# A mixer and expert network in one kernel: the expert stage rebuilt around ranked experts and light blocks, block copies on GpSimd

## The chip, the cores and the metric

One core of a Trainium2 chip runs the whole program. The metric is the device time of one execution in microseconds; the time of the kernel before is the median of 3 runs. Engines are called PE (TensorE), DVE (VectorE), ACT (ScalarE), GpSimd (POOL in the profile) and SP (SyncE).

## What is computed

The reference takes 256 tokens of width 1024 through two blocks. The first (two layers of a SwiGLU network, a mixer of a short convolution and a gated recurrence, and another SwiGLU network) and the attention and recurrence of the second are not touched. The change is in the last part of the second block, a hierarchical mixture of 16 experts:

```python
g_logits = hf @ w_rg + b_rg
g_top = argmax(g_logits)                      # one of 4 groups
e_in = (hf @ w_re + b_re)[group g_top]        # its 4 experts
top_v, top_j = lax.top_k(e_in, 2)             # two experts a token
for e in range(16):
    he = silu(hf @ w1[e]) * (hf @ w3[e])      # 1024 -> 512
    y = y + combine[:, e:e + 1] * (he @ w2[e])  # 512 -> 1024
x = x + g2 * y
```

All is fp32. So 512 rows (256 tokens, 2 experts each) are to be worked on, spread over 16 experts as the data have it; the kernel must be right for every spread.

## The kernel before

Every fp32 product of weights is taken as three products of fp32r halves: hi x hi, hi x lo, lo x hi. Weights come from memory in units of 1 MB (128 x 2048). For a unit ACT writes the rounded half (`expert_hi`, L1124) and DVE the remainder (`expert_lo`, L1544: raw minus hi). Six raw buffers (RAWS) and four pairs of split buffers (SPLITS) are used in turn: a fetch waits for the split that frees its raw buffer, a split waits until PE has used the unit four before.

An expert has six units: 0 and 1 for w1, 2 and 3 for w3, 4 and 5 for w2. The order of units interleaves two neighbours: the four of block b come, then the last two of block b - 1 (`expert_unit`).

Routing. After the norm, PE computes the router's logits, DVE picks group and experts, PE counts and ranks by a product with a triangular matrix (L861 to L865), and DVE makes from it each row's place among the 512 rows sorted by expert (L1620 to L1632). One-hot matrices of these places (`first_one_hot`) select the rows: PE multiplies the split hidden states with them (`gather`, L882), ACT and DVE write the outcome to `xsel` (`select`, L1161 and L1716), transposed, hi and lo, 512 columns. The first 256 columns are made before the first product, the other 256 within block 0.

Blocks. There are 19 blocks of 128 slots: one for each expert in the order of numbers, and three extra ones for experts with more than 128 rows, whose numbers and offsets DVE works out during blocks 1 to 3 (`extra_counts`, `extra_places`, `extra_experts`). The weights of the 16 first blocks lie in a known order, so their fetches begin before the routing is known; the three extra ones are fetched by an index that SP reads. GpSimd copies a block's 128 columns from `xsel` (at an offset that it reads from `offs`) to one of two buffers in `xT` (`columns`, L609); block 0 is taken from `xsel` itself.

On PE the order is, for block b: units 0 and 1 (gate, bank 0), the turn of the hidden rows of block b - 1 (four transposes, L908), units 2 and 3 (up, bank 1), then the outputs of block b - 1 (units 4 and 5, L926 to L928, banks 3 and 4). A unit of a product is 12 matmuls of 512 columns (L897 to L899). ACT takes the silu (L1174), DVE the product with up (L1791), ACT and DVE split the turned hidden rows (L1186, L1782), and ACT and DVE write the output rows to `ybuf` (L1202, L1808; DVE multiplies its half by the gate vector). GpSimd stores `ybuf` to `yd` in memory (L591). At the end, GpSimd gathers each token's two rows from `yd` by index (L624), and DVE adds them with their weights (`near_sum`); rows of the last two blocks (FAR and FAR + 1) are not gathered but added by a product with one-hot shares (`far_products`, L946).

`idle(n)` and `keep_busy(n)` on PE are matmuls on zeros between these steps.

Of the kernel before, what the change touches and what calls it, by code (L numbers as in the profile page):

```python
# [23 lines left out]
I32 = mybir.dt.int32  # L24
# [40 lines left out]
EXTRA = (2 * T) // (SLOTS + 1)  # L65
BLOCKS = EXPERTS + EXTRA
BATCH = 2 * SLOTS
BATCHES = 2
LAST_OFFSET = 2 * T - SLOTS
# [3 lines left out]

FAR = BLOCKS - 2
FAR_SLOT = FAR * SLOTS
# [3 lines left out]
PICK_FILL, PLACE_FILL = 20, 12  # L79
# [23 lines left out]
def constants():  # L103
# [12 lines left out]
            "c_before": (s < t).astype(np.float32), "c_iota": np.arange(BATCH, dtype=np.float32)}  # L116
# [53 lines left out]
def expert_unit(b, j):  # L170

    if j < 4:
        return j + (6 * b - 2 if b else 0)
    return 6 * b + (4 + j if b < BLOCKS - 1 else j)


UNIT_OF = {expert_unit(b, j): (b, j) for b in range(BLOCKS) for j in range(6)}
assert sorted(UNIT_OF) == list(range(6 * BLOCKS))  # L180
# [7 lines left out]
def build(nc, t, out):  # L188
    ctx = ExitStack()
    with ctx:  # L190
# [55 lines left out]
        def xT_banks(i):  # L246
# [94 lines left out]
        before = sb("before", [P, P], F32, route)  # L341
        iota = sb("iota", [P, BATCH], F32, route)
        counts = sb("counts", [P, 8, EXPERTS], F32, route)
        extra = sb("extra", [P, 3, EXTRA, EXPERTS], F32, route)
# [6 lines left out]
        emap = sb("emap", [P, EXTRA], I32, route)  # L351
# [8 lines left out]
        oneh0 = sb("oneh0", [P, TT, BATCH], F32R, moe)  # L360
        far = sb("far", [P, TT, 2], F32, moe)
        share = sb("share", [P, 2, TT, SLOTS], F32, moe)
        tests = sb("tests", [P, 2, BATCH], F32, moe)
        oneh1 = sb("oneh1", [P, TT, BATCH], F32R, moe)
# [11 lines left out]
        oneh = [oneh0, oneh1]  # L376
# [5 lines left out]
        xcur = [xT[:, 4 * n:4 * n + 4].rearrange("p k a t -> p (k a t)").rearrange("p (m s) -> p m s", s=SLOTS)  # L382
                for n in range(2)]
# [64 lines left out]
            "rw_hi rw_split routeT_ps routeT route_ps rexp_in rexp rexp2_in rexp2 "  # L448
            "tables_in h2_hi h2_lo picked rank_ps begins extras xcur slots weighed oneh0 oneh "
# [45 lines left out]
        def stored_to(b):  # L495


            return 16 * (b // 2 + 1)
# [22 lines left out]
        def sp_block2(sp):  # L521
            for p in range(6 * BLOCKS):
                b, j = UNIT_OF[p]
# [10 lines left out]
                if b < EXPERTS:  # L534
                    src = t["experts"][b * 6 + j:b * 6 + j + 1, :, :]
                else:
                    if j == 0:
                        if b == EXPERTS:
                            sp.wait_ge(ev["extras"], 1)
                            expert = 0  # L540
                        m = b - EXPERTS
                        expert, last = sp.value_load(emap[0:1, m:m + 1], min_val=0, max_val=EXPERTS - 1), expert
                    e = expert if j < 4 or b == BLOCKS - 1 else last
                    src = t["experts"][bass.ds(e * 6 + j, 1), :, :]
# [8 lines left out]
        def pool_block2(pool):  # L553
# [31 lines left out]
            g = nc.gpsimd  # L585

            def store(b):

                pool.wait_ge(ev["y_left"], b + 1)
                pool.wait_ge(ev["y_right"], b + 1)  # L590
                pool.dma_start(t["yd"][b * SLOTS:(b + 1) * SLOTS, :], ybuf[:, b % 2, :]).then_inc(stored[b % 2], 16)  # L591
# [6 lines left out]
            def columns(b):  # L598


                pool.wait_ge(*((ev["begins"], 1) if b < EXPERTS else (ev["extras"], 1)))
                offset = pool.value_load(offs[0:1, b:b + 1], min_val=0, max_val=LAST_OFFSET)
                if b == 1:
                    pool.wait_ge(xT_ps, XT_DONE + 8 * BATCHES)
                    pool.wait_ge(xThi_done, XT_DONE + 4 * BATCHES)
                    pool.wait_ge(xTlo_done, XT_DONE + 4 * BATCHES)
                if b >= 3:
                    pool.wait_ge(*expert_used(expert_unit(b - 2, 3) + 1))
# [2109 lines left out]
```

## Time and profile before

| | us |
|---|---|
| runs (3) | 1888.61, 1890.15, 1888.44; median 1888.61 |
| profiled execution, first to last instruction | 1885.4 |
| PE busy | 1815.4 (96%) |
| DVE busy | 1446.7 (77%) |
| ACT busy | 982.6 (52%) |
| GpSimd busy | 118.2 (6%) |

For the profiled execution the profile has its span alone; the runs lie 3.0 to 4.8 us above it. Times within the kernel are counted from the span's start. The expert stage is its last fifth. The clock column of a stretch is the TensorE clock that was granted, 1.00 for 2.4 GHz and 0.50 for 1.2 GHz. A group's "idle before" is time in which the engine stood still ahead of these instructions, and behind the arrow stands what ended it.

### The profile page before, as it was taken

Reading aid. Unit: us, or ns where it says so; the run is one execution under the profiler, and the core shown is the slowest. Engines: PE = TensorE matmul, PEld = TensorE weight load, DVE = VectorE, ACT = ScalarE, POOL = GpSimd, SP = SyncE. Lnnn points to the kernel's source line nnn. Section 1 sums busy time; section 2 is a strip of 40 time slices with the busy share of each in tenths; the row PEclk is TensorE's granted clock in tenths of the full one; section 3 lists DMA queues with packets and bytes.
Section 4 is the critical chain, followed back from the end, with each engine's and each line's share of the span. In section 5 each row is a group of like instructions: output and inputs, shape, how many; then the busy total and the mean of one; then the engine's idle time right before and its main releaser. Section 6 shows DMA issues by size and latency. Waiting matters only on the chain.

```text
span 1885.4 us, 28170 instructions
## 1 busy us (share of the span) xinstructions
PE 1815.4 (96%) x10912; PEld 1597.0 (85%) x10912; DVE 1446.7 (77%) x1543; ACT 982.6 (52%) x932; POOL 118.2 (6%) x116
## 2 busy tenths in 40 slices
PE   7999999999999999999999999998998899999998
PEld 6888899998888788889999978886997777777876
DVE  7555786857877765567877687779588889999998
ACT  4444465534444454446464345443435456767774
POOL 1000000000000000000000000001000011212222
PEclk9999999999999999999999999998999999999999
DMA  6555455564777465545546557774432359999995
GB/s 250 190 188 196 161 179 179 201 224 144 280 252 259 157 216 185 200 156 181 199 164 245 176 186 279 248 260 144 140 136 90 103 185 373 367 373 391 389 385 217
DMA packets 61615, 417.14 MB, mean 221 GB/s; under 512 B 7288, under 2 KB 7664, under 8 KB 13648
## 3 DMA queue, kind: packets, MB, share of 16 engines
q1 hardware_dynamic: 51392, 369.19, 54.4%
q0 software_dynamic: 10112, 46.59, 7.3%
q8 instruction: 70, 1.15, 0.2%
q14 instruction: 25, 0.20, 0.0%
q10 hardware_dynamic: 16, 0.01, 0.0%
HBM read 405.79 MB, written 9.98 MB: 221 GB/s over the span
## 4 chain that ended last, share of the span: by engine, by line
PE 80%; DVE 11%; DVEq 3%; issue 3%; ACT 1%; ACTq 1%; DMA 0%; POOL 0%; POOLq 0%
PE ps L1916 14%; PE ps L1915 7%; PE ps L1900 7%; PE ps L1902 7%; PE ps L1901 7%; PE ps L2017 4%; PE ps L2018 4%; PE ps L2021 4%; PE ps L899 3%; PE ps L897 3%; PE ps L898 3%; PE ps L926 2%; PE ps L1913 2%; DVE wlo L2350 2%; PE ps L928 2%
## 5 line engine op out<-in xcount | busy, mean ns | idle before, releaser
L2350 DVE TENSOR_TENSOR wlo<-raw,whi 128x2048 fp32r<-128x2048 f32 x236 | 538.2, 2289 | 194.0 <-ACT whi L2182 191.2
L2182 ACT ACTIVATE whi<-raw 128x2048 fp32r<-128x2048 f32 x236 | 451.1, 1912 | 271.6 <-PE ps L1902 112.7
L1916 PE MATMUL ps<-xT,whi 128*128 128x512 f32 x1232 | 440.4, 397 | 0.0
L1915 PE MATMUL ps<-xT,wlo 128*128 128x256 f32 x1232 | 344.6, 280 | 0.1
L1916 PEld LDWEIGHTS ps<-xT,whi 128*128 128x128 f32 x1232 | 231.9, 188 | 47.6
L1900 PE MATMUL ps<-xT,whi 128*128 128x256 f32 x928 | 263.5, 284 | 2.0 <-DVE xT L2361 2.0
L1901 PE MATMUL ps<-xT,whi 128*128 128x256 f32 x928 | 263.2, 284 | 0.0
L1902 PE MATMUL ps<-xT,wlo 128*128 128x256 f32 x928 | 263.1, 284 | 0.0
L1915 PEld LDWEIGHTS ps<-xT,wlo 128*128 128x128 f32 x1232 | 233.0, 189 | 8.9 <-DVE xT L2369 1.0
L1544 DVE TENSOR_TENSOR wlo<-raw,whi 128x2048 fp32r<-128x2048 f32 x76 | 201.3, 2661 | 10.6 <-ACT whi L1124 9.9
L2206 ACT ACTIVATE rest<-ps 128x512 f32<-128x512 f32 x88 | 52.7, 599 | 251.9 <-PE ps L1916 251.9
L1900 PEld LDWEIGHTS ps<-xT,whi 128*128 128x128 f32 x928 | 178.8, 193 | 2.2 <-DVE xT L2361 2.2
L1901 PEld LDWEIGHTS ps<-xT,whi 128*128 128x128 f32 x928 | 178.8, 193 | 0.0
L1902 PEld LDWEIGHTS ps<-xT,wlo 128*128 128x128 f32 x928 | 178.7, 193 | 0.0
L1124 ACT ACTIVATE whi<-raw 128x2048 fp32r<-128x2048 f32 x76 | 145.6, 1918 | 47.9 <-PE ps L928 30.5
L2017 PE MATMUL ps<-whi,hhi 128*128 128x512 f32 x288 | 112.4, 390 | 2.1 <-DVE wlo L2350 2.1
L897 PE MATMUL ps<-whi,xT 128*128 128x512 f32 x288 | 113.9, 395 | 0.0
L899 PE MATMUL ps<-whi,xT 128*128 128x512 f32 x288 | 112.4, 390 | 0.0
L898 PE MATMUL ps<-wlo,xT 128*128 128x512 f32 x288 | 112.2, 390 | 0.0
L2018 PE MATMUL ps<-wlo,hhi 128*128 128x512 f32 x288 | 112.1, 389 | 0.0
L1544 DVE TENSOR_TENSOR wlo<-mod,whi 128x2048 fp32r<-128x2048 f32 x38 | 87.4, 2299 | 2.3 <-ACT whi L1124 2.2
L2021 PE MATMUL ps<-whi,hlo 128*128 128x512 f32 x288 | 88.7, 389 | 0.0
(516 smaller groups left out, 3288.1 us busy)
## 6 DMA issues: line engine op xcount, KB each, us to landing
raw<-stream SPq DMA_DIRECT2D x236, 1024.0 KB, 4.9
raw<-experts SPq DMA_DIRECT2D x76, 1024.0 KB, 7.2
mod<-experts SPq DMA_DIRECT2D x38, 1024.0 KB, 6.7
adaraw<-ada POOLq DMA_DIRECT2D x24, 1024.0 KB, 5.1
yd<-lnrow POOLq DMA_DIRECT2D x17, 512.0 KB, 8.7
lnrow<-ln_g POOLq DMA_DIRECT2D x6, 512.0 KB, 4.8
lnrow<-ln_b POOLq DMA_DIRECT2D x6, 512.0 KB, 6.3
x_sb<-x SPq DMA_DIRECT2D x1, 1024.0 KB, 5.1
```

The source lines that it names most:

```text
L897: mm(o, h, wh[:, rs], start=k == 0, stop=False)
L899: last = mm(o, lo, wh[:, rs], start=False, stop=k == KD - 1)
L1544: v.tensor_tensor(splits[p % SPLITS][1], raws[p % RAWS], splits[p % SPLITS][0].bitcast(F32), ALU.subtract).then_inc(lo_done, 1)
L1900: nc.tensor.matmul(outs[tile], wh, xh[:, k, :], start=k == 0, stop=False)
L1901: nc.tensor.matmul(outs[tile], wh, xl[:, k, :], start=False, stop=False)
L1902: last = nc.tensor.matmul(outs[tile], wl, xh[:, k, :], start=False, stop=k == KD - 1)
L1915: nc.tensor.matmul(bank(b, T), wl, xThi[:, k, :], start=False, stop=False)
L1916: return nc.tensor.matmul(bank(b), wh, both, start=False, stop=k == KD - 1)
L2017: nc.tensor.matmul(o, h, whi[:, slot, c:c + 512], start=start and k == 0, stop=False)
L2018: nc.tensor.matmul(o, h, wlo[:, slot, c:c + 512], start=False, stop=False)
L2182: act_fn(whi[:, slot, :], raw[:, slot, :], ACT.Copy).then_inc(hi_done, 1)
L2350: v.tensor_tensor(wlo[:, slot, :], raw[:, slot, :], whi[:, slot, :].bitcast(F32), ALU.subtract).then_inc(lo_done, 1)
```

## The change

The expert stage is rebuilt. The experts are ranked by their counts: the expert of rank r has at most min(256, 512 / (r + 1)) rows. So it is fixed how many blocks each rank needs, and how wide: ranks 0 and 1 have two blocks of 128 slots, rank 2 one of 128 and one of 64, ranks 3 to 6 one of 128, ranks 7 to 15 one of 64. These are 9 wide and 10 light blocks for 16 experts, and each expert's weights are fetched once, by an index that SP reads after the sort. RANK_AT gives the order in which ranks are worked on: 0, 7, 8, 9, 1, 10, 11, 12, 2, 13, 14, 15, 3, 4, 5, 6.

In a light block a stationary tile holds 64 columns of the hi half and 64 of the lo half side by side, and two matmuls (with the hi and the lo weights) take the place of three; the two halves of the outcome's partitions are added later, for gate and up by an fp32 matmul with two stacked unit matrices (`fold`), for the rows out by ACT and DVE. Both batches of `gather` come before the first product. GpSimd copies the columns of all blocks, of block 0 too, into three buffers (two in `xT`, one in the one-hot matrices' place), in the order columns(q + 2), then the stores of expert q.

```diff
+LIGHT = 64
+RANK_AT = [0, 7, 8, 9, 1, 10, 11, 12, 2, 13, 14, 15, 3, 4, 5, 6]
+def rows_at_most(rank):
+
+    return min(T, 2 * T // (rank + 1))
+def widths(q):
+
+    left = rows_at_most(RANK_AT[q])
+    out = []
+    while left > 0:
+        out.append(LIGHT if left <= LIGHT else SLOTS)
+        left -= out[-1]
+    return out
...
+COLUMNS_AT = {0: (0, 1), 4: (0, 1), 8: (0, 1), 1: (2,), 2: (0,), 3: (2,), 5: (2,), 6: (0,), 7: (2,), 9: (2,), 10: (0,),
+              11: (2,), 12: (0,), 13: (1,), 14: (0,), 15: (1,)}
-PICK_FILL, PLACE_FILL = 20, 12
+PICK_FILL, PLACE_FILL, FIRST_FILL = 20, 20, 12
...
         def sp_block2(sp):
+                if j == 0:
+                    if q == 0:
+                        sp.wait_ge(ev["sorted"], 1)
+                        expert = 0
+                    expert, last = sp.value_load(emap[0:1, q:q + 1], min_val=0, max_val=EXPERTS - 1), expert
+                e = expert if j < 4 or q == EXPERTS - 1 else last
+                src = t["experts"][bass.ds(e * 6 + j, 1), :, :]
                 sp.dma_start(raws[p % RAWS], src.rearrange("o p n -> p (o n)")).then_inc(expert_loaded(p)[0], 16)
...
+            def columns(q):
+                if q == 0:
+                    pool.wait_ge(ev["begins"], 1)
                     pool.wait_ge(xThi_done, XT_DONE + 4 * BATCHES)
                     pool.wait_ge(xTlo_done, XT_DONE + 4 * BATCHES)
+                for n, m, width in BLOCKS_OF[q]:
+                    of = q if m == 0 else EXPERTS + RANK_AT[q]
+                    offset = pool.value_load(offs[0:1, of:of + 1], min_val=0, max_val=2 * T - width)
+                    users = [b for b in range(n) if BUFFER_OF[b] == BUFFER_OF[n]]
+                    if users:
+                        pool.wait_ge(*expert_used(expert_unit(BLOCK[users[-1]][0], 3) + 1))
+                    nc.gpsimd.tensor_copy(xcur(n), xsel[:, :, :, bass.ds(offset, width)]).then_inc(ev["xcur"], 1)
+
+            columns(0)
             columns(1)
+            for q in range(EXPERTS):
+                if q + 2 < EXPERTS:
+                    columns(q + 2)
+                for n, _, _ in BLOCKS_OF[q]:
+                    if n < FAR:
+                        store(n)
...
+            def product(q, j):
+                for n, m, width in BLOCKS_OF[q]:
+                    o = bank((G_BANK if j < 2 else U_BANK)[m])
+                    for r in range(4):
+                        k = 4 * (j % 2) + r
+                        rs = slice(r * D_EXPERT, (r + 1) * D_EXPERT)
+                        if width == SLOTS:
+                            h, lo = (xcur(n)[:, part, k, :] for part in range(2))
+                            mm(o, h, wh[:, rs], start=k == 0, stop=False)
+                            mm(o, h, wl[:, rs], start=False, stop=False)
+                            last = mm(o, lo, wh[:, rs], start=False, stop=k == KD - 1)
+                        else:
+                            both = light_columns(n, k)
+                            mm(o, both, wh[:, rs], start=k == 0, stop=False)
+                            last = mm(o, both, wl[:, rs], start=False, stop=k == KD - 1)
...
+            def turn_hidden(n):
+                    pe.wait_ge(silu_done, FFN_DONE + n + 1)
+                    pe.wait_ge(ev["ucopy"], LIGHT_NO[n] + 1)
+                    for a, rows_in_two in enumerate((gated, hide)):
+                        for f in range(4):
+                            c = (4 * a + f) * LIGHT
+                            last = mm(o[:, c:c + LIGHT], rows_in_two[:, f * P:(f + 1) * P], fold, start=True, stop=True)
...
+            for c in range(BATCHES):
+                for group in range(8):
+                    gather(c, group)
+            idle(FIRST_FILL)
+            for q in range(EXPERTS + 1):
+                if q >= 1:
+                    turn_hidden(first_block(q - 1))
+                if q < EXPERTS:
+                    pe.wait_ge(ev["xcur"], last_block(q) + 1)
...
+                    product(q, 0)
+                    product(q, 1)
...
+                if q >= 1 and len(BLOCKS_OF[q - 1]) > 1:
+                    turn_hidden(last_block(q - 1))
+                if q < EXPERTS:
+                    product(q, 2)
+                    product(q, 3)
+                if q >= 1:
+                    outputs(q - 1, 4)
+                    outputs(q - 1, 5)
...
+            def block_offsets():
+                v.tensor_tensor(sort2[:, :, :], perm[:, :, :], across_q(begin), ALU.mult)
+                dve.drain()
+                v.tensor_reduce(begin_q, sort2[:, :, :], AX_X, ALU.add)
+                dve.drain()
+                v.tensor_tensor(offs[:, 0:EXPERTS], begin_q, last_at, ALU.min)
...
+            first_one_hot(1)
+            block_offsets()
+            for pair in range(4):
+                select(1, pair)
+            for p in range(SPLITS):
+                expert_lo(p)
...
+            def turned_hidden(n):
+                dve.wait_ge(ev["silT"], LIGHT_NO[n] + 1)
+                both, product = light_hidden(m), hide[:, 0:4 * LIGHT]
+                v.tensor_tensor(product, gated[:, 0:4 * LIGHT], bank(T_BANK[m], 4 * LIGHT, 8 * LIGHT),
+                                ALU.mult).then_inc(hid_done, 1)
+                dve.drain()
...
+                v.tensor_copy(both[:, 0], product).then_inc(hhi_done, 1)
+                dve.drain()
+                v.tensor_tensor(both[:, 1], product, both[:, 0].bitcast(F32), ALU.subtract).then_inc(hlo_done, 1)
+            def rows_out(n):
+                if width == LIGHT:
+                    dve.wait_ge(ev["y_left"], n + 1)
+                    v.tensor_tensor(ybuf[0:LIGHT, n % 2, :], ybuf[0:LIGHT, n % 2, :], banks(Y_BANK[m], 2)[0:LIGHT, :],
+                                    ALU.add).then_inc(ev["y_right"], 1)
...
-                if half == 0:
-                    v.tensor_tensor(acc, acc, row(mod, 5)[:, cs], ALU.mult)
-                    dve.drain()
+                v.tensor_tensor(acc, acc, row(mod, 5)[:, cs], ALU.mult)
+                dve.drain()
```

The sort itself is two comparisons of all pairs of experts (16 x 16 = 256 elements) and their sums on DVE, between the counts and the first one-hot matrix; the steps for second blocks follow in the rounds of experts 1 to 4, the shares of far rows in rounds 10 and 11. The splits of units 0 to 3 on ACT and DVE, which stood within the norm and the routing, come after both batches. DVE's order in the round of expert q is: the turned hidden rows of expert q - 1, two splits, routing work, a split, the product rows of expert q, a split, a split, the rows out of expert q - 1, a split.

## Rows read from the trace of the kernel before

**Rows 1.** Busy time by stretch (count), clock, DMA share, GB/s.

```profile
1550.11:1690.50 140.39, 131.29 (x582) 105.45 (x581) 134.91 (x106) 98.61 (x70) 26.80 (x14) 1.00 0.98 368
1690.50:1850.00 159.50, 157.09 (x696) 126.27 (x695) 154.05 (x83) 118.28 (x82) 33.53 (x18) 1.00 1.00 390
```

**Rows 2.** Waits, 1550 to 1850 us: total us, times, longest.

```profile
PE ps L926 <- issue: 10.2, 15, 1.4
DVE wlo L1544 <- ACT whi L1124: 9.2, 32, 0.4
```

**Rows 3.** Timeline of DVE, one block: start us, us, engine, line, operation.

```profile
1709.60 2.29 DVE L1544 TENSOR_TENSOR wlo<-raw,whi 128x2048 fp32r<-128x2048 f32 x1 [0.20 <-ACT whi L1124]
...
1711.81 0.68 DVE L1808 TENSOR_TENSOR lnrow<-ps,mod 128x512 f32<-128x512 f32 x1
1712.89 6.22 DVE L1544 TENSOR_TENSOR wlo<-raw,whi 128x2048 fp32r<-128x2048 f32 x2 [0.39 <-ACT whi L1124]
...
1724.04 0.67 DVE L1791 TENSOR_TENSOR mod<-mod,ps 128x512 f32<-128x512 f32 x1
...
1727.11 2.29 DVE L1544 TENSOR_TENSOR wlo<-raw,whi 128x2048 fp32r<-128x2048 f32 x1 [0.20 <-ACT whi L1124]
```

**Rows 4.** GpSimd's copies: first two together (timeline), all (duration ns min/median/max).

```profile
1541.51 5.85 POOL L609 CAST xT<-xsel 128x2048 fp32r x2 [48.11 <-DVE xsel L1716]
...
L609 POOL CAST xT<-xsel x18: 1914/3228/3981, 1541.5 to 1836.0; 128x2048 fp32r x18
```

**Rows 5.** Timeline of PE: first product, block 17, outputs.

```profile
1528.94 0.47 PE L897 MATMUL ps<-whi,xsel 128*128 128x512 f32 x1 [0.83 <-ACT xsel L1161]
...
1849.95 0.39 PE L897 MATMUL ps<-whi,xT 128*128 128x512 f32 x1
...
1855.40 0.60 PE L936 MATMUL ps<-eye,tests 128*128 128x128 f32 x4
1855.84 0.60 PE L908 MATMUL ps<-eye,mod 128*128 128x128 f32 x4
...
1861.75 0.39 PE L926 MATMUL ps<-whi,hThi 128*128 128x512 f32 x1
```

**Rows 6.** Timeline of PE, fp32 matmuls of 64 columns, after a gap and later.

```profile
1456.79 1.09 PE L771 MATMUL ps<-eye,lnrow 128*128 128x128 f32 x8 [3.32 <-ACT lnrow L1076]
1459.10 3.67 PE L779 MATMUL ps<-av,qk 128*128 128x64 f32 x16 [1.22 <-DVE xT L1406]
...
1479.57 1.89 PE L779 MATMUL ps<-av,qk 128*128 128x64 f32 x16
```

**Rows 7.** Timeline of DVE between the counts and the first product.

```profile
1520.03 0.19 DVE L1620 TENSOR_TENSOR_SCAN counts<-ones,ps 128x16 f32<-128x16 f32 x1 [0.47 <-PE ps L865]
...
1523.42 1.22 DVE L1606 TENSOR_TENSOR xT<-cat,xT 128x1024 fp32r<-128x1024 f32 x1
...
1528.15 0.69 DVE L1716 CAST xsel<-ps 128x512 fp32r<-128x512 f32 x1 [0.27 <-PE ps L882]
```

**Rows 8.** Timeline of the end: PE and SP.

```profile
1867.35 0.60 PE L908 MATMUL ps<-eye,mod 128*128 128x128 f32 x4
...
1880.33 2.91 SPq L550 DMA_DIRECT2D out<-x_sb  x4
```

**Rows 9.** DVE by shape: busy us, mean ns, idle before.

```profile
L1464 DVE TENSOR_TENSOR cat<-ps,nrm 128x256 f32<-128x256 f32 x2 | 0.8, 420 | 0.1
...
L1643 DVE TENSOR_SCALAR mod<-iota,sit 128x256 f32<-128x256 f32 x2 | 0.6, 349 | 0.1
...
L1475 DVE COPY qk<-ps 128x512 f32<-128x512 f32 x2 | 1.3, 686 | 0.6 <-PE ps L771 0.6
...
L1394 DVE TENSOR_TENSOR lg<-ps,score 128x1024 f32<-128x1024 f32 x2 | 2.4, 1222 | 0.1
```

**Rows 10.** DMA, 1550 to 1850 us: all, and the fetches of a unit.

```profile
DMA packets 16777, 113.96 MB, mean 380 GB/s; under 512 B 1854, under 2 KB 1854, under 8 KB 3902
...
raw<-experts SPq DMA_DIRECT2D x67, 1024.0 KB, 7.2
```

More of the change, by code:

```diff
@@ L521, in sp_block2 @@
         def sp_block2(sp):
-            for p in range(6 * BLOCKS):
-                b, j = UNIT_OF[p]
+            for p in range(6 * EXPERTS):
+                q, j = UNIT_OF[p]
                 if p < RING:
@@ new lines, in act_block2 @@
+            for c in range(BATCHES):
+                for pair in range(4):
+                    select(c, pair)
+            for p in range(SPLITS):
+                expert_hi(p)
+            for q in range(EXPERTS + 1):
+                two = q >= 1 and len(BLOCKS_OF[q - 1]) > 1
+                if q >= 1:
+                    turned_hidden(first_block(q - 1))
+                if two:
+                    gate_rows(last_block(q - 1))
+                if q < EXPERTS:
+                    freed(q, 0)
+                    freed(q, 1)
+                if two:
+                    turned_hidden(last_block(q - 1))
+                if q < EXPERTS:
+                    gate_rows(first_block(q))
+                    if q == EXPERTS - 1:
@@ L1665, in extra_counts @@
                 dve.drain()
-                v.tensor_tensor_scan(counts[:, 6, :], ones[:, 0:EXPERTS], many, 0.0, ALU.mult, ALU.add)
+                v.tensor_reduce(begin_q, sort2[:, :, :], AX_X, ALU.add)
                 dve.drain()
-            def extra_places():
-                for m in range(EXTRA):
-                    v.scalar_tensor_tensor(extra[:, 0, m, :], counts[:, 6, :], float(m + 1), many, ALU.is_equal, ALU.mult)
-                v.scalar_tensor_tensor(counts[:, 7, :], counts[:, 6, :], float(SLOTS), off_x, ALU.mult, ALU.subtract)
+                v.tensor_tensor(offs[:, 0:EXPERTS], begin_q, last_at, ALU.min)
@@ L1720, in dve_block2 @@
                 select(0, pair)
-            expert_lo(2)
             first_one_hot(1)
-            expert_lo(3)
+            block_offsets()
+            for pair in range(4):
+                select(1, pair)
+            for p in range(SPLITS):
+                expert_lo(p)
             def weights():
@@ new lines, in dve_block2 @@
+            for q in range(EXPERTS + 1):
+                two = q >= 1 and len(BLOCKS_OF[q - 1]) > 1
+                if q >= 1:
+                    turned_hidden(first_block(q - 1))
+                if two:
+                    product_rows(last_block(q - 1))
+                if q < EXPERTS:
+                    freed(q, 0)
+                    freed(q, 1)
+                if two:
+                    turned_hidden(last_block(q - 1))
+                if q == 1:
+                    steps_of_first_blocks()
+                elif q == 2:
+                    steps_of_second_blocks()
+                elif q == 3:
+                    choice_rows()
+                elif q == 4:
@@ L2567, in _ @@
             dve.drain()
+            dve.wait_ge(eye_in, 16)
+            v.tensor_tensor(fold, eye[:, 0:LIGHT], eye[:, LIGHT:], ALU.add)
             dve.wait_ge(bada_in, 16)
```

458 lines of the change are left out of this document (237 added, 221 removed).

## The prediction

> **What bounds the kernel now.** I read the table by stretch first, then the waits, then one block on VectorE (DVE), then PE, GpSimd and the DMA. The expert stage runs from PE's first product at 1528.94 us to 1867.35, where the last block's hidden rows are turned: 338.4 us for 18 of 19 rounds [rows 5, 8]. In it PE, DVE and DMA are all nearly full [rows 1]: no engine has much room, and only less work can make it shorter. What paces a round is DVE. Between two equal points of successive blocks (1709.60 and 1727.11) lie 17.5 us [rows 3], filled by six splits of weights at 2.2 us, three pieces of block work at 0.61, 1.7 us by which GpSimd's copy lengthens a split (the pair takes 6.22 where two alone take 4.5), and 0.6 us of waits for ACT. The same copy takes 3.23 us by the median [rows 4]. In the first half, where small routing work lies between the splits, PE is busy 131.3 of 140.4 us, later 157.1 of 159.5 [rows 1], and its waits stand at the outputs [rows 2]. PE needs 12 matmuls of 512 columns a unit: 24 in 5.45 us is 0.228, and at the outputs 0.233 [rows 5]; I take 0.2314, so 2.78 us a unit, and 16.7 a block with 0.45 for the turn, close behind DVE's 17.5. DMA moves 380 GB/s there and 1 MB lands in 7 us [rows 10]; nobody waits for it.
>
> **What the change does, part by part.** Removed: the three extra experts' 18 units (114 become 96). There are 9 wide blocks of 128 slots and 10 light ones of 64. A light block needs 8 matmuls a unit, where a wide one needs 12. Added: two blocks in experts 0 and 4 (both wide) and 8 (wide and light) of the new order, a sort of experts before the first fetch, fp32 matmuls against the fold in every light block, more DVE work in a light block, and a first expert that waits for both of its copies.
>
> **Cost of one expert.** PE, wide: 16.7 + 0.45. PE, light: 48 x 0.2314 = 11.1, and eight fp32 matmuls of 64 columns; eight such took 1.89 us at full clock [rows 6], so 13.0. PE, two wide: 5.55 us a unit, 33.3. DVE, light: six splits 13.3; a 512-wide copy out of PSUM 0.61; product, copy and difference at 256 wide, 0.42, 0.35 and 0.42 with their drains 1.3; a 1024-wide add with PSUM 1.15 [rows 9], each less the 0.07 by which neighbours overlap; together 3.05. The copy of 64 slots is half of the wide one, so I take half its toll, 0.9 (0 if it falls beside other work, 1.7 at most). Sum 17.2: **a light expert is DVE-paced**, and saves PE time that nobody needs. A double expert is PE-paced. Lights cost no less than a wide block did before; what is won is that three whole rounds go, and part of it goes back to the doubles.
>
> **Schedule of the stage,** counted from the first product. Four split units stand between DVE and PE, so DVE enters each light run with a lead and lags PE in each double.
> Expert 0's products: 4 x 5.55 = 22.2.
> Experts 1 to 4: the fourth split in the ring ends 4.1 later (a split of ACT 1.9 and of DVE 2.2 after the unit is freed). DVE then has expert 1's round: 13.3, block work 3.65 (two blocks of expert 0), toll 0.9, routing steps with 256-wide operations 2.2, so 20.0; expert 2's: 13.3 + 3.05 + 3.4 for two wide copies + 1.0, so 20.7. In the next round it needs 11.2 until PE has turned block 3 (light work 1.3, three splits 6.6, routing 0.8, copy 0.6, fold 1.9), then PE is alone on the path: 22.2 for expert 4's products and 3.7 for expert 3's outputs. Sum 81.9.
> Experts 5 to 8: DVE lags 6.1 behind, 1.6 and 0.5 of waits, rounds of 18.8 and 18.9, 10.4 until the turn, 4 x 4.63 + 3.7 for the double with one light block. 78.5.
> Experts 9 to 12: 6.1 + 1.0, rounds of 19.0, 19.2 and 19.2 (the shares of far rows, 1.2 each, and wide copies), then 1.3 + 4.4 + 1.9, so 72.0. Experts 13 to 15 are wide, at the 17.5 of now: 52.5.
> Sum 22.2 + 81.9 + 78.5 + 72.0 + 52.5 = 307.1, against 338.4: **31.3 won**.
>
> **The start.** Fetches no longer run ahead. From the counts (1520.03) to the last copy of the gathered rows now takes until 1528.84, and the first product follows [rows 7]. The sort adds five dependent 256-wide steps and a cast, less what now lies there: 1.7 us; two splits that no longer stand ahead of the routing give 0.35 back. So the first gather ends at 1530.2. The second one-hot (six 256-wide operations, 2.2 [rows 9]) and the second gather (5.4, as from 1523.42 to 1528.84) must now come before the first product: 1537.8. Then GpSimd reads its offset (0.3) and copies two wide blocks, which took 5.85 together beside splits [rows 4]: first product at about 1544.0, 15.1 later. The first unit is issued on SP at about 1524, so its landing (7 us) and split hide behind this; with that cover gone it would cost up to 8. The twelve fillers on PE last 2.8, so about 3.3 us are idle. After such a gap (3.32) the clock went to half and the same matmuls took 3.67 where 1.89 is full [rows 6]. I take 3 us for it, bounds 0 and 5. A copy by itself takes 1.91 at least [rows 4]; two of those instead of 5.85 give the low bound, 2 us earlier.
> On this copy the Trainium skill (GPSIMD Engine Reference, Elementwise — side-by-side cycle accounting and Engine selection) says that one-input work runs near line rate there, 1.03 cycles an element; at 1.2 GHz a wide copy would be an estimated 1.8 us, and the start 2 us earlier. The trace agrees only with its shortest copy; beside splits the measurement decides.
>
> **The end.** From the last turn (1867.35) to the end of the span 18.05 us are left; its last instructions are the stores of the output [rows 8]. The gate factor is now applied in all four near sums, two more 512-wide products of 0.69 [rows 9] and a drain ahead of the last rows out of PSUM, 1.5 in all: 19.55. The store of rows and the gathers keep their place; no price.
>
> **Sum against the profiled span of 1885.4:** +15.1 (start) + 3 (clock) - 31.3 + 1.5 = -11.7, so 1873.7. The runs shown lie 3.0 to 4.8 above that span, their median 3.2; so 1888.6 - 11.7 = 1876.9. A measurement of this kernel can tell about 0.2% (3.8 us) from no change.
>
> **The rivals.**
> *The ring gives no lead (slower).* Place: the hand-over from a double expert to the lights. DVE works in program order, and in the double it also waits for PE before each piece. If it comes out of a double without split units in hand, the four units (8.8 us) of each of three light runs are paid again: +26, or 1903. It decides from 12 us lost, less than half of the lead. For: all DVE work is in one queue, and PE already waited at its outputs when DVE had a little more to do [rows 2]. Against: PE's units are 5.55 us there, DVE's and ACT's 4.1. 0.12.
> *The clock falls in the light runs (slower).* PE is busy 13.0 of 17.2 us there, with gaps up to 1.7. If every light expert ran at half clock it would need 26 and pace the run, 9 x 9 = +80; PE would then be full, which brings the clock back, so I take a third, +27: 1904. For it speaks the fall after the 3.32 us gap [rows 6]; against, that no single gap is as long. 0.06.
> The Trainium skill (TensorE: Matmul & The Clock Gate, HAM oscillation) tells of a kernel whose bursts shorter than their waits fell back to the low clock at every tile; the gap in the trace agrees, and no row shows it for gaps as short as these.
> *DVE is cheaper than I say (faster).* The copies fall into its idle time in the doubles, half tolls vanish (10 x 0.9), the light work is 2.5 instead of 3.05 (5) and the clock stays up (3): -17, or 1860. For: in the doubles DVE has 20 to 30 us to spare. Against: copies come after the rows are stored, at the head of a round. 0.16.
> *The wins just cover the start (no change).* A first product 5 us later than I say, and a quarter of the no-lead case (6.5): 1888.4. 0.14.
>
> **How the numbers follow.** The forecast (1866 to 1885) has 0.52. Faster by over 0.2%, so under 1884.8: 0.52 + 0.16 = 0.68. Within: 0.14. Slower: 0.12 + 0.06 = 0.18. The predicted time is the first case's, 1877. The range 1857 to 1896 reaches the cheap-DVE case and the middle of the no-lead case, and takes in the bounds of tolls (9 each way), start (2 to 8) and clock.
>
> **What would show it.** Right: 96 splits of DVE; first product near 1544 after two copies; products of expert 0 in 22.2 us; in light runs DVE has hardly any idle time and PE idles a quarter; a light expert every 17 us; in doubles DVE waits for ACT, and ACT for PE. Wrong: light experts at 15 us or below, or at 20 and more; PE's clock under 1.0 within them; ACT waiting for DMA; a first product before 1540 or after 1550.

## The result and the profile after

The changed kernel takes 1901.74 us (median, 1900.68 to 1902.75), the kernel before 1888.53 (1887.86 to 1890.15): a ratio of 1.0071, interval 1.0059 to 1.0083. The forecast of 1877 and its range (1857 to 1896) were wrong, and so was the sign. The profiled span is 1900.7 us, against 1885.4 before.

The start first. Timelines of DVE, GpSimd and PE of the changed kernel (start us, us, engine, line, operation):

```profile
1522.38 0.17 DVE L1747 SCALAR_TENSOR_TENSOR counts<-ps,sorts 128x16 f32<-128x16 f32 x1 [0.25 <-PE ps L933]
...
1540.10 0.69 DVE L1862 CAST xsel<-ps 128x512 fp32r<-128x512 f32 x1 [0.36 <-PE ps L950]
...
1541.87 5.81 POOL L677 CAST xT<-xsel 128x2048 fp32r x2 [44.89 <-issue]
...
1547.74 0.70 PE L967 MATMUL ps<-whi,xT 128*128 128x512 f32 x1 [4.92 <-POOL xT L677]
```

The counts stand at 1522.38, 2.35 us later than in [rows 7]. The kernels of the experiments, which compute the same up to there, have them at 1518.3 to 1522.0, so most of this is the spread between executions. From the counts to the first product it is 25.4 us, where the forecast had 1544.0 - 1520.03 = 24.0. The two wide copies take 5.81 together, as in [rows 4]. So, from the counts on, the start is as forecast but for 1.4 us.

The stage, from that product to the last turn at 1882.71, took 335.0 us against 338.4 before and 307.1 forecast. This is the table by stretch (us, busy us of PE, of its weight loads, DVE, ACT and GpSimd with counts, granted clock, DMA share, GB/s). Experts are counted from 0 in the new order. The stretches end where the first block of expert 4, of 8, of 12 and of 15 is turned:

```profile
1547.74:1660.33 112.59, 102.42 (x440) 82.51 (x441) 84.06 (x70) 58.16 (x42) 13.88 (x10) 0.94 0.78 282
1660.33:1747.69 87.36, 75.82 (x330) 60.76 (x329) 68.92 (x52) 53.47 (x40) 11.40 (x10) 0.92 0.84 306
1747.69:1825.46 77.77, 69.04 (x301) 55.63 (x300) 69.85 (x54) 54.68 (x41) 11.92 (x9) 0.91 0.89 329
1825.46:1882.71 57.25, 53.22 (x233) 43.31 (x233) 49.35 (x28) 37.40 (x27) 29.66 (x9) 0.97 0.84 319
```

The forecast had 104.1, 78.5, 72.0 and 52.5 for them: each is 5 to 9 us longer. Against [rows 1], DVE has fallen from nearly full to 0.75 to 0.90 of a stretch, the clock from 1.00 to as low as 0.91, and DMA from 368 and 390 GB/s to between 282 and 329. So the work did get less, and no engine is full over a whole stretch any more: something is waited for. At a clock of 0.94, 0.92, 0.91 and 0.97, twice what is missing is half clock (1.2 instead of 2.4 GHz): 13.5 + 14.0 + 14.0 + 3.4 = 45 us of the stage.

The waits name it. First the list for 1550 to 1850 us (total, times, longest), then PE's timeline at the places:

```profile
DVE wlo L1662 <- ACT whi L1215: 45.5, 18, 6.1
ACT whi L1215 <- PE ps L969: 44.7, 16, 10.0
...
PE ps L993 <- DVE mod L1924: 10.0, 6, 3.4
...
PE ps L967 <- DVE lnrow L1958: 7.3, 2, 3.7
```

```profile
1633.11 0.68 PE L967 MATMUL ps<-whi,xT 128*128 128x512 f32 x1 [3.66 <-DVE lnrow L1958]
1633.59 0.63 PE L968 MATMUL ps<-wlo,xT 128*128 128x512 f32 x1
...
1637.30 0.40 PE L969 MATMUL ps<-whi,xT 128*128 128x512 f32 x1
...
1667.98 1.09 PE L986 MATMUL ps<-eye,mod 128*128 128x128 f32 x4 [3.39 <-DVE mod L1920]
...
1722.98 0.77 PE L967 MATMUL ps<-whi,xT 128*128 128x512 f32 x1 [3.67 <-DVE lnrow L1958]
...
1755.34 1.91 PE L993 MATMUL ps<-spt,mod 128*128 128x64 f32 x11 [3.40 <-DVE mod L1924]
...
1847.07 0.50 PE L967 MATMUL ps<-whi,xT 128*128 128x512 f32 x1 [4.02 <-POOL xT L677]
```

In [rows 2] DVE waited 9.2 us for ACT, here 45.5; and ACT waits 44.7 for PE to free a unit. PE itself waits at five places of 3.4 to 4.0 us: before the products of experts 4 and 8 for the stored rows, before the turn of the second block of each for its product rows, and once, at expert 14, for GpSimd. Behind the first of them a product starts every 0.43 us instead of every 0.23, for some 3.5 us. The same happens in light experts, behind shorter waits:

```profile
1607.86 2.33 PE L993 MATMUL ps<-spt,mod 128*128 128x64 f32 x16 [1.71 <-DVE mod L1924]
...
1610.52 0.63 PE L973 MATMUL ps<-wlo,onehs 128*128 128x512 f32 x1
```

Where DVE stands idle is seen when the stage is cut into its light runs and its double experts (the same columns as above; first light run, the double expert 4, last light run):

```profile
1577.10:1633.11 56.01, 47.22 (x212) 37.86 (x213) 52.37 (x46) 36.92 (x28) 7.38 (x6) 0.94 0.90 334
1633.11:1667.98 34.87, 31.48 (x132) 25.51 (x133) 20.79 (x21) 17.36 (x12) 4.89 (x4) 0.94 0.64 225
1755.34:1808.07 52.73, 48.13 (x201) 38.67 (x201) 44.99 (x37) 35.00 (x27) 6.51 (x5) 0.87 0.87 321
```

DVE is busy 0.94 and 0.85 of these light runs, and 0.60 of the double.

The wait at expert 14 is one copy, the last but one of GpSimd's copies. GpSimd's timeline, and DVE's beside it:

```profile
1796.14 2.76 POOL L677 CAST xT<-xsel 128x2048 fp32r x1
...
1814.64 2.79 POOL L677 CAST xT<-xsel 128x2048 fp32r x1
...
1832.04 14.98 POOL L677 CAST xT<-xsel 128x2048 fp32r x1
```

```profile
1830.77 2.28 DVE L1662 TENSOR_TENSOR wlo<-raw,whi 128x2048 fp32r<-128x2048 f32 x1
1832.97 0.68 DVE L1933 TENSOR_TENSOR hTlo<-ps,hThi 128x512 fp32r<-128x512 f32 x1
1833.57 2.27 DVE L1662 TENSOR_TENSOR wlo<-raw,whi 128x2048 fp32r<-128x2048 f32 x1
...
1840.17 0.67 DVE L1920 TENSOR_TENSOR mod<-mod,ps 128x512 f32<-128x512 f32 x1
...
1842.97 2.28 DVE L1662 TENSOR_TENSOR wlo<-raw,whi 128x2048 fp32r<-128x2048 f32 x1
1845.18 0.68 DVE L1961 COPY lnrow<-ps 128x512 f32<-128x512 f32 x1
1845.78 3.38 DVE L1662 TENSOR_TENSOR wlo<-raw,whi 128x2048 fp32r<-128x2048 f32 x1
```

The same copy took 2.76 and 2.79 us an expert or two earlier, and 14.98 here. In those 15 us no DVE row carries a wait, and no split is lengthened (2.27 to 2.28) until the copy out of PSUM at 1845.18, behind which the split takes 3.38 and the copy ends. Two pieces that read one operand from PSUM and one from SBUF (1832.97, 1840.17) stand in between and did not let it in. The end of the kernel is as before: 1900.7 - 1882.71 = 18.0 us from the last turn.

### The profile page after: what moved, and what is told of

Its sections match the earlier page's. It is cut to its first block, busy times and chain, and to the rows that moved or that the text cites. A ratio compares the mean times of both kernels' runs of the same rounds, so it can differ in the third digit from the quotient of the medians.

```text
span 1900.7 us, 28124 instructions
## 1 busy us (share of the span) xinstructions
PE 1802.2 (95%) x10812; PEld 1586.7 (83%) x10812; DVE 1407.2 (74%) x1555; ACT 948.1 (50%) x914; POOL 115.4 (6%) x118
## 4 chain that ended last, share of the span: by engine, by line
PE 73%; DVE 13%; DVEq 4%; issue 4%; ACT 3%; POOL 1%; ACTq 1%; DMA 0%; POOLq 0%
PE ps L2114 14%; PE ps L2113 7%; PE ps L2098 7%; PE ps L2100 7%; PE ps L2099 7%; PE ps L2215 4%; PE ps L2216 4%; PE ps L2219 4%; DVE wlo L1662 2%; PE ps L2111 2%; DVE wlo L2548 2%; PE ps L967 2%; PE ps L968 1%; PE ps L969 1%; DVE mod L2670 1%
## 5 line engine op out<-in xcount | busy, mean ns | idle before, releaser
L2548 DVE TENSOR_TENSOR wlo<-raw,whi 128x2048 fp32r<-128x2048 f32 x236 | 538.3, 2290 | 196.5 <-ACT whi L2380 194.0
L2380 ACT ACTIVATE whi<-raw 128x2048 fp32r<-128x2048 f32 x236 | 450.8, 1911 | 275.8 <-PE ps L2100 113.7
L1662 DVE TENSOR_TENSOR wlo<-raw,whi 128x2048 fp32r<-128x2048 f32 x64 | 152.2, 2380 | 41.8 <-ACT whi L1215 41.6
L2404 ACT ACTIVATE rest<-ps 128x512 f32<-128x512 f32 x88 | 52.5, 597 | 253.1 <-PE ps L2114 253.1
L1215 ACT ACTIVATE whi<-raw 128x2048 fp32r<-128x2048 f32 x64 | 122.2, 1913 | 81.2 <-PE ps L969 38.0
L1662 DVE TENSOR_TENSOR wlo<-mod,whi 128x2048 fp32r<-128x2048 f32 x32 | 73.1, 2284 | 12.1 <-ACT whi L1215 12.1
L2670 DVE SCALAR_TENSOR_TENSOR mod<-adaraw,csil_now,mod 128x512 f32 (+1 forms) x96 | 72.2, 752 | 11.1 <-issue 5.4
L2583 DVE TENSOR_TENSOR sil<-ps,rest 128x512 f32<-128x512 f32 x44 | 30.4, 692 | 62.9 <-ACT rest L2404 62.9
L967 PE MATMUL ps<-whi,xT 128*128 128x512 f32 x144 | 59.8, 415 | 16.3 <-POOL xT L677 8.9
```

Source lines behind the costliest of these rows:

```text
L1215: act_fn(splits[p % SPLITS][0], raws[p % RAWS], ACT.Copy).then_inc(hi_done, 1)
L1662: v.tensor_tensor(splits[p % SPLITS][1], raws[p % RAWS], splits[p % SPLITS][0].bitcast(F32), ALU.subtract).then_inc(lo_done, 1)
L2380: act_fn(whi[:, slot, :], raw[:, slot, :], ACT.Copy).then_inc(hi_done, 1)
L2548: v.tensor_tensor(wlo[:, slot, :], raw[:, slot, :], whi[:, slot, :].bitcast(F32), ALU.subtract).then_inc(lo_done, 1)
```

## Experiments

All are timed in 3 rounds beside the kernel before, which had medians of 1887.85 to 1888.3 us in them. They fall in two groups: the waits and the copies (e1, e3 to e10), and the clock (e2, e11 to e16). Where a recorded expectation puts the long copy at expert 15, it is the copy for expert 14.

**e1: wait only for what is read.** A double expert's second block writes banks that only the second block before it had in use; the kernel of the change waits for the rows of every block up to the one two places back, that of expert q - 2. e1 waits for the rows of the last second block alone.

```diff
-                        pe.wait_ge(ev["y_left"], first_block(q) - 1)
-                        pe.wait_ge(ev["y_right"], first_block(q) - 1)
+                        seconds = [n for n in range(first_block(q)) if BLOCK[n][1] == 1]
+                        pe.wait_ge(ev["y_left"], seconds[-1] + 1)
+                        pe.wait_ge(ev["y_right"], seconds[-1] + 1)
```

> The wait of a double expert's first product is moved from the rows of the expert two before to the rows of the last second block, which is what its banks need. Theory (the late rows cost time): in the changed kernel PE stood 3.66 and 3.67 us there, right ahead of PE-paced rounds, so both go, 7.3 us, and with them some of the half clock that follows; 1892 to 1895 against 1901.7. Rival (DVE paces these rounds, so PE only waits elsewhere): 1900 to 1902, with the waits turned up in front of the outputs.

Measured: 1889.0 us, ratio 1.0005 (0.9995 to 1.0014). That is 12.7 us under the change, more than the theory had; the rival falls. The two waits were 7.3 us. Most of the rest is the half clock behind them, by e13 below.

**e3: a narrow copy.** GpSimd copies 8 of a block's columns; the products of the others read what stood there, so that the expert outputs are left out.

```diff
-                    nc.gpsimd.tensor_copy(xcur(n), xsel[:, :, :, bass.ds(offset, width)]).then_inc(ev["xcur"], 1)
+                    nc.gpsimd.tensor_copy(xcur(n)[:, :, :, 0:8], xsel[:, :, :, bass.ds(offset, 8)]).then_inc(ev["xcur"], 1)
```

> GpSimd copies 8 columns of each block in place of all; the rest of each block is left out. Theory (copies cost at the start, by their tolls on DVE and once by standing 15 us): start 5 us earlier, 4 us at the copy of the last buffer, tolls of at most 24 us of DVE time of which about half is on the path: 1875 to 1885. Rival (copies hide, doubles and waits are all of the loss): only the start's 5 us and the 4 us go, 1892 to 1893.

Measured: 1886.29 us, ratio 0.9987 (0.9977 to 0.9996), between the two. GpSimd's timeline, and PE's behind the long copy:

```profile
1802.95 1.17 POOL L677 CAST xT<-xsel 128x128 fp32r x1
...
1819.11 13.37 POOL L677 CAST xT<-xsel 128x128 fp32r x1
...
1834.13 1.15 POOL L677 CAST xT<-xsel 128x128 fp32r x1
```

```profile
1832.54 0.50 PE L967 MATMUL ps<-whi,xT 128*128 128x512 f32 x1 [2.09 <-POOL xT L677]
```

The copy for expert 14 moves a sixteenth of the data and still stands for 13.37 us. So its length is not work; it stands still. PE waits 2.09 us for it, where it waited 4.02, and the waits for stored rows (3.7 each) and for the second blocks' product rows (3.4 each) are all there: that is what keeps e3 above its theory.

**e4, e5: the copies on ScalarE (ACT),** which leaves DVE's splits at 2.28 to 2.29 us (e8's rows below); e5 has e1's wait as well.

```diff
-                    nc.gpsimd.tensor_copy(xcur(n), xsel[:, :, :, bass.ds(offset, width)]).then_inc(ev["xcur"], 1)
...
+                    act_fn(xcur(n), xsel[:, :, :, bass.ds(offset, width)], ACT.Copy).then_inc(ev["xcur"], 1)
```

The copies of experts 0 and 1 stand before ACT's splits of units 0 and 2, those of expert q + 2 at the end of round q.

> The same copies on ACT, one round ahead, in place of GpSimd. ACT has a third of the stage idle; a wide copy should take 1.92 us there and lengthen no split. Theory (GpSimd's copies take DVE's time and once keep PE waiting): the tolls and the 4 us wait go, 1880 to 1892. Rival (the copies delay ACT's own halves of the splits, which is as bad): 1900 to 1906.

> Two parts at once: TensorE waits at experts 4 and 8 for the rows of the last second block alone (that by itself gave 1889.0), and the copies of the columns are done by ScalarE (that by itself gave 1889.2). Theory (each removed wait lies on the path, and they are different stretches of it): 1901.7 - 12.7 - 12.5 = 1876, range 1873 to 1880. Rival (TensorE goes at the pace of the splits of the weights, and whatever is taken out is waited for at the next split): 1886 to 1889.

Measured: e4 1889.24 (1.0008, 0.9998 to 1.0017), e5 1877.75 (0.9951, 0.9934 to 0.9968). Each alone is worth 12.5 to 12.7 us, both 24.0: they add up, and the theory of waits in series holds against the one of a pace that takes everything back. In e4 the first product waits for something else, the split of its weights, which now begins behind the copies:

```profile
1549.23 0.77 PE L948 MATMUL ps<-whi,xT 128*128 128x512 f32 x1 [6.97 <-DVE wlo L1663]
```

**e6: a gap for the copy.** e1, and behind DVE's split of a wide block's turned rows:

```diff
+                    dve.drain()
```

> As the wait kernel (1889.0), with GpSimd's copies, and a drain of VectorE after the split of a wide block's turned activations, so that VectorE has a gap once in each expert. Theory (a copy gets in only at a gap, and without one it stood for 15.0 us at expert 15): that copy takes 3 to 5 us, TensorE's wait of 4.0 us for it goes, and the time is 1883 to 1886. Rival (the length of that copy has another cause, or the pace there is that of the splits anyway): 1888 to 1890.

Measured: 1882.79 (0.997, 0.9959 to 0.9981), 6.2 under e1. GpSimd's copies for experts 14 and 15, and DVE beside the first:

```profile
1819.72 2.78 POOL L677 CAST xT<-xsel 128x2048 fp32r x1
...
1835.86 2.77 POOL L677 CAST xT<-xsel 128x2048 fp32r x1
```

```profile
1820.64 0.67 DVE L1934 TENSOR_TENSOR hTlo<-ps,hThi 128x512 fp32r<-128x512 f32 x1
1821.48 3.17 DVE L1663 TENSOR_TENSOR wlo<-raw,whi 128x2048 fp32r<-128x2048 f32 x1 [0.16 <-issue]
```

With a gap of 0.16 us the copy goes through: 2.78 us instead of 14.98, for 0.9 us on the next split. It is as short in the other three profiles with this drain (e9, e15, e16). Single executions scatter by 3 to 4 us, and the two profiled ones are only 2.4 apart; the 6.2 is the difference of the medians of 10 and 7 runs, which do not overlap.

**e7: the first split earlier.** e5, and ACT splits unit 0 between the two batches of gathered rows.

> As the kernel with both (e5), and ScalarE splits the first unit of weights ahead of its copies of the second batch of gathered tokens instead of behind them. In the ScalarE kernel the first product waited 6.97 us for VectorE's part of that first unit. Theory: the first product starts 3 to 4 us earlier, and all of it is kept: 3 to 4 us under e5. Rival (splits pace the stage in its first experts): under 1 us of it is kept.

Measured: 1871.66 (0.9917, 0.99 to 0.9933), 6.1 under e5; the first product is at 1542.53 instead of 1547.35, 4.8 earlier. All of it is kept; the 1.3 us beyond it are not secured, as the four runs of each kernel lie up to 5.6 us apart.

**e8, e10: the turn of a second block later.**

```diff
-                if q >= 1 and len(BLOCKS_OF[q - 1]) > 1:
-                    turn_hidden(last_block(q - 1))
                 if q < EXPERTS:
                     product(q, 2)
                     product(q, 3)
+                if q >= 1 and len(BLOCKS_OF[q - 1]) > 1:
+                    turn_hidden(last_block(q - 1))
```

> As e7, and TensorE turns the activations of a second block after the fourth unit's products of the next expert instead of between the second and the third. Theory (the waits of 3.4 us ahead of that turn at experts 5 and 9, and what there is of it at expert 1, are hand-over time that two more units hide): 6 to 9 us under e7. Rival (VectorE stands at the turn that now comes later and releases the next units later by as much): within 2 us of e7, or slower.

> The change as it stands, with nothing but the later turn of a second block. Theory (the waits are in series): 9 us under the change, 1891 to 1895. Rival (the waits of 3.7 us at experts 4 and 8 follow from the same rows, which now come later still, and take it back): 1899 to 1902.

Measured: e8 1862.23 (0.9865, 0.9848 to 0.9881), 9.4 under e7; e10, the change with this alone, 1890.9 (1.0006, 0.9994 to 1.0018), 10.8 under it (three of its ten runs lie at 1885.6 to 1886.0, seven at 1890.1 to 1893.5). In e10 the waits for the rows stay as they were (3.67 at expert 4). Something is taken back at the outputs, where PE waits 10.7 us for split weights instead of 7.2, but less than the waits for product rows that go. **e8 beats both kernels**, the one before by 26 us. Its table by stretch, cut at the same turns:

```profile
1543.13:1644.72 101.59, 96.04 (x441) 77.68 (x442) 79.89 (x70) 70.46 (x51) 2.17 (x4) 1.00 0.83 312
1644.72:1719.98 75.26, 71.02 (x329) 56.54 (x328) 66.02 (x52) 58.44 (x45) 2.72 (x5) 1.00 0.94 354
1719.98:1791.21 71.23, 66.24 (x301) 53.18 (x300) 68.07 (x54) 58.85 (x44) 2.70 (x5) 0.95 0.95 362
1791.21:1842.54 51.33, 51.33 (x233) 42.11 (x232) 46.98 (x28) 41.24 (x30) 7.86 (x6) 1.00 0.86 342
```

The stage takes 299.4 us: 101.6, 75.3, 71.2 and 51.3 where the forecast had 104.1, 78.5, 72.0 and 52.5.

**e9: all mends, copies on GpSimd.**

> The four mends at once with the copies still on GpSimd: the wait for the last second block's rows alone, the drain of e6, the first unit split ahead of the second batch's copies by ScalarE, the second block turned after the fourth unit. Against the same with the copies on ScalarE (1862.2). Theory (GpSimd's copies lengthen VectorE's splits by some 14 us in all and VectorE is near the pace of the stage): 1870 to 1875, of 1882.8 (e6) about 9 less. Rival (with the 15 us copy gone, it no longer matters who copies): 1861 to 1864.

Measured: 1875.54 (0.993, 0.9912 to 0.9948); copies on ACT without the drain are worth 13.3 us over copies on GpSimd with it, in the mended schedule. A part is the start, where the earlier split lengthens the copies that PE waits for (6.80 for the two, and the first product at 1546.07). The rest, 9.9 us of the stage (309.3 against 299.4), goes with the tolls that DVE pays: PE waits 11.7 us for split weights at the outputs in e9, and 3.9 in e8. DVE's groups of the change, then of e8 (busy us, mean ns, idle before):

```profile
L1662 DVE TENSOR_TENSOR wlo<-raw,whi 128x2048 fp32r<-128x2048 f32 x64 | 152.2, 2380 | 41.8 <-ACT whi L1215 41.6
L1662 DVE TENSOR_TENSOR wlo<-mod,whi 128x2048 fp32r<-128x2048 f32 x32 | 73.1, 2284 | 12.1 <-ACT whi L1215 12.1
...
L1945 DVE CAST hThi<-mod 128x256 fp32r<-128x256 f32 x9 | 8.5, 949 | 0.8
L1947 DVE TENSOR_TENSOR hThi<-mod,hThi 128x256 fp32r<-128x256 f32 x9 | 6.0, 671 | 1.0 <-issue 0.3
```

```profile
L1667 DVE TENSOR_TENSOR wlo<-raw,whi 128x2048 fp32r<-128x2048 f32 x64 | 146.2, 2285 | 23.2 <-ACT whi L1197 23.0
...
L1952 DVE TENSOR_TENSOR hThi<-mod,hThi 128x256 fp32r<-128x256 f32 x9 | 3.8, 425 | 1.0 <-issue 0.3
L1950 DVE CAST hThi<-mod 128x256 fp32r<-128x256 f32 x9 | 2.7, 295 | 0.8
```

In the change the tolls of all copies are 6.0 on the splits, 5.8 on the light blocks' copy and 2.2 on their difference: 14 us (in e9 the same groups, with the splits of both kinds of buffers, come to 14 as well). More than half fell on short pieces of light block work, which PE waits for next; of the 6.0, some 4 fell on three splits beside the first two copies (10.82 us together). That the tolls are all of the 9.9 is argued, not isolated: the drain, too, is in e9 alone.

**e2, e13, e14: does the clock cost?** Products of zeros on TensorE (0.23 us each), 14 ahead of the rows' wait at experts 4 and 8 (e13), 8 ahead of the outputs of each expert with a single light block, nine in all (e14), or both (e2):

```diff
+            def hold(count):
+                for _ in range(count):
+                    mm(bank(7), zero_w[:, :], zero_w[:, :].unsqueeze(1).to_broadcast([P, 4, P]), start=True, stop=True)
...
+                        hold(14)
                         pe.wait_ge(ev["y_left"], first_block(q) - 1)
...
+                    if len(BLOCKS_OF[q - 1]) == 1 and BLOCK[first_block(q - 1)][2] == LIGHT:
+                        hold(8)
                     outputs(q - 1, 4)
```

> Matmuls on zeros are put into PE's gaps: 14 ahead of the products of the double experts 4 and 8 (3.2 us of 3.7 us waited there), 8 ahead of the outputs of every light expert (1.8 us). Theory (half clock after gaps costs PE-paced rounds several us): the clock stays at 1.00 in the light runs and the time falls by 3 to 8 us, to 1894 to 1899. Rival (half clock falls where DVE paces anyway): the clock rises as well but the time stays or gets longer by what the fillers delay, 1901 to 1910.

> The change with fourteen products of zeros on TensorE ahead of its wait for rows at experts 4 and 8 alone, one half of e2 (which gave 1896.0 with both halves; the change 1901.7). Theory (what e2 won, 5.7 us, is the half clock right behind the waits of 3.7 us, where TensorE's products are what all wait for): 4 to 6 us of it, so 1896 to 1898. Rival (it is the many light waits): 1900 to 1902.

> The change with eight products of zeros ahead of each light expert's outputs alone, the other half of e2. Theory (in light experts TensorE has slack, so the half clock there costs nothing, as the fill of e11 gave 0.7 us): 1900 to 1902. Rival (it is the many light waits): 1896 to 1898.

Measured: e2 1896.02 (1.0047, 1.003 to 1.0063), e13 1895.45 (1.0034, 1.002 to 1.0048), e14 1900.04 (1.0059, 1.0043 to 1.0076). PE's timeline in e13 at expert 4:

```profile
1628.12 3.46 PE L901 MATMUL ps<-zero_w 128*128 128x512 f32 x14
1631.82 0.47 PE L972 MATMUL ps<-whi,xT 128*128 128x512 f32 x1 [0.24 <-issue]
1632.13 0.39 PE L973 MATMUL ps<-wlo,xT 128*128 128x512 f32 x1
```

The rows are waited for as long as ever, but the products behind them run at full clock: 6.3 us won, 3 at each place. The copy for expert 14 stands for 14.97 us as before, so it plays no part in this. The light half wins 1.7.

**e11, e12, e15, e16: the clock in light experts.** e11 is e1 with 8 such products in each of the nine light experts, e12 is e8 with 5, e15 and e16 are e6 with 8 and 4.

> The wait kernel (1889.0, 31 us at half clock within the stage) with eight products of zeros on TensorE ahead of each light expert's outputs, where it waits some 3 us anyway; the output is the same. Theory (the half clock comes from these light waits and a part of it is on the path): the half clock in the stage falls to under 12 us and the time by 3 to 7 us, to 1882 to 1886. Rival (the products run at half clock while TensorE has slack, so the clock costs nothing): 1888 to 1890, with the clock up.

> The fastest so far (e8, 1862.2, 10 us at half clock) with five products of zeros on TensorE ahead of each light expert's outputs. Theory: the waits there are now mostly under 1 us, so that the products (0.21 to 0.24 us each, ten light experts) cost more than the clock gives: 1863 to 1869. Rival (the clock still costs there): 1858 to 1861.

> e6 (the mended wait and the drain, 1882.8) with eight products of zeros ahead of each light expert's outputs. In e11 and e14 those products also made GpSimd's 15 us copy a short one, worth some 6 us by e6, so their small gains (0.7 and 1.7) hide a loss. Here that copy is short with and without them. Theory (the half clock in light experts costs next to nothing, the products cost their own time): 1886 to 1890, with the clock up. Rival (the clock there costs as much as the products): 1881 to 1884.

> As e15 with four such products instead of eight: 0.9 us an expert, which lie nearly all within TensorE's waits. Theory: 1881 to 1884, no gain beyond 1.5 us from whatever the clock does. Rival (the half clock in light experts is on the path): 1876 to 1880.

Measured: e11 1888.28 (1.0, 0.999 to 1.0009), e12 1865.14 (0.9876, 0.9859 to 0.9894), e15 1889.12 (1.0004, 0.9995 to 1.0014), e16 1886.33 (0.9989, 0.9979 to 0.9998). e2, e11 and e14 decide less than they seemed to: in all three, GpSimd's copy for expert 14 took 2.8 us instead of 15. Why is open. In e11 the DVE rows beside it, counted from the copy's start, lie as in the change to 0.01 us and show no gap, yet here the split gives way:

```profile
1822.01 2.78 POOL L677 CAST xT<-xsel 128x2048 fp32r x1
```

```profile
1823.54 3.40 DVE L1670 TENSOR_TENSOR wlo<-raw,whi 128x2048 fp32r<-128x2048 f32 x1
```

Where that copy is short anyway, 4 products an expert cost 3.5 us (e16, 0.10 us for each of 36) and 8 cost 6.3 (e15, 0.09 for each of 72). I had thought that four of them would lie within TensorE's waits; they do not. The clock of 1545 to 1865 us is 0.95 in e6 and in e16, and 0.97 in e15. If each product costs the same in both, 72 cost 7.1, so going from 0.95 to 0.97 gave back under 1 us. That is as far as fillers can tell: they delay the outputs by their own time, and no run takes the half clock away without them. So it is argued, not shown, that the half clock in light experts costs hardly anything.

## Why the prediction was wrong

*The start* (+15.1, to 1544.0) was right within 1.4 us, counted from the counts, and so was its mechanism: PE waits for two copies of 5.81 us together. In the profiled execution the counts themselves came 2.4 us later.

*The schedule of the stage* (307.1) is the step that failed, not by its prices but by what it left out: it measured 335.0, 27.9 more. With the waits mended and the copies still on GpSimd (e9) the stage takes 1855.38 - 1546.07 = 309.3 us and the kernel 1875.5, against the forecast's 307.1 and 1877. Three events were missing:
- "PE is alone on the path" in a double expert. It was not: the code makes it wait for the rows of the block two back, which DVE stores late. 12.7 us (e1): 7.3 of waiting, some 6 of half clock behind it (e13).
- "until PE has turned block 3" counted the hand-over from DVE to PE once. The second block has another, 3.4 us with nothing on PE to cover it: 9.4 to 10.8 us with the clock behind it (e8, e10). In e9 this and the earlier split won 7.3 together.
- A copy that stands still for 15 us: 6.2 (e6). [Rows 4] showed 3981 ns as the longest, so nothing in the trace before gave it away.

Together 12.7 + 6.2 + 7.3 = 26.2, which is the difference between 1901.7 and 1875.5 by construction; that this lands within 1.5 us of the forecast is partly luck, since the tolls were put too high. I had 9 x 1.7 + 10 x 0.9 = 24.3 and they are 14, so some 10 us of other costs lie unnamed in the 309.3, perhaps the clock among them (0.97 over e9's stage).

*"A light expert is DVE-paced."* This held for the most part. DVE is busy 0.94, 0.89 and 0.85 of the three light runs, against 0.60 and 0.62 of the doubles at experts 4 and 8. In the first run DVE's rounds last 20.2 and 19.6 us (from one copy of the up rows to the next: 1586.79, 1607.03, 1626.65), where the forecast had 20.0 and 20.7. DVE's 54 us of waits for ACT (41.8 + 12.1) stand mostly in the doubles and in expert 0 (34 us), 11 in the light runs, 7 in the last experts.

*The clock term* (+3, bounds 0 to 5) had the fall at the start alone. There it cost about 1.5: expert 0's products took 23.7 us instead of 22.2. 45 us of the stage ran at half clock. What counts is where: behind a wait that everybody shared it cost 6.3 us (e13), in the light experts under a microsecond for what e15 gave back, by the argument above. The rival of the clock in light runs had the event right: it fell behind a wait of 1.71 us (1607.86 above), which its "against" (no gap as long as 3.32) had ruled out; its price of 27 was, by that argument, far too high. The Trainium skill (TensorE: Matmul & The Clock Gate, HAM oscillation) describes a kernel whose clock falls back in the waits between short bursts of matmuls; the trace agrees, with 0.91 to 0.94 in the first three stretches where [rows 1] have 1.00.

*The rival of the ring without a lead* (1903) names nearly the time that came, but not the way: it had PE kept waiting in the light runs by DVE without split units in hand, for 26 us. PE waited for split weights 7.2 us in all, at the outputs alone.

*The end* (+1.5) came to 0 (18.0 us from the last turn against 18.05): the two extra products hid.

*Of the signs to look for*, "PE's clock under 1.0 within them" came true, as did, in part, "at 20 and more": the first round of each light run took 20.2 to 22.6 us.

## What to carry to other kernels

When a schedule is worked out from rates, list every semaphore wait that the code puts in front of the engine you call "alone on the path", with who satisfies it and when; a wait written as "block n - 2" may be stricter than what it protects. The three rounds of work that were saved show up only when the hand-overs between the others are covered: here 12.7, 6.2 and 7.3 us of mends turned 13 us lost into 13 us won, and the copies on an engine that doesn't slow the others into 26.

## What the runs showed of the hardware

A GpSimd copy beside DVE's splits, which read two operands from SBUF, made no progress for up to 15 us: 14.98 us for 128x2048, and 13.37 us for 128x128, which takes 0.29 to 1.94 otherwise. A drain on DVE, a gap of 0.16 us, went with 2.78 to 2.79 in all four profiles that have it. In the five profiles without drain and without fillers in light experts (the change, e1, e3, e10, e13) the copy was long; in the three with such fillers and no drain (e2, e11, e14) it was short, with no gap in DVE's rows. In the long cases it got in at a DVE copy that reads PSUM alone (1845.18 in the change), and not behind pieces that read PSUM and SBUF; in e11 it did get in behind one of those (the turned rows, then the split of 3.40). So what exactly lets it in is open. The Trainium skill (GPSIMD Engine Reference, Key points) states that GpSimd shares its SBUF interfaces with VectorE and contends with instructions of two SBUF inputs; the runs agree, with 14.98 us in place of 2.8. The toll goes to whichever DVE instruction the copy meets: 0.4 to 1.1 us on single splits of the changed kernel, 0.65 us on average on a cast of 256 columns that takes 0.29 alone.

The same copies on ACT (e8) left DVE's splits at 2.28 us and its casts at 0.29.
